# Streaming encoder step on one core: the gather of the sample heads in the bank of the transposes, the row sums on GpSimd, and a place of its own for one row tile

## The reference, cut to what matters

```
for l in range(2):
    p = rmsnorm(x, g_norm[l]) @ w_in[l]
    o_a = sparse attention (top 256 keys of an indexer), o_b = forgetting attention,
    o_c = chunk-band attention, o_m = cross-attention into 256 memory tokens   # 4 heads of 64 each
    x = x + concat(o * silu(own gate columns of p)) @ w_out[l]                 # 1024 x 1024
y = rmsnorm(x, g_final)
```

## Time and profile before

| | us |
|---|---|
| median of 3 runs | 1720.25 |
| the profiled execution | 1722.64 |
| its span | 1720.8 |
| PE busy in the span | 1664.0 |
| DVE busy | 1094.3 |
| ACT busy | 626.3 |
| POOL busy | 301.4 |

### The profile page before, as it was taken

The page is one execution under the profiler, slowest core; times in us unless marked ns, Lnnn a source line. Parts: engine busy times, 40 slices in busy tenths (PEclk is TensorE's granted clock), DMA queues, the critical chain, the costliest instruction groups (busy, mean ns, idle before and its releaser), DMA issues.

```text
span 1720.8 us, 28357 instructions
## 1 busy us (share of the span) xinstructions
PE 1664.0 (97%) x9815; PEld 1120.9 (65%) x9815; DVE 1094.3 (64%) x2845; ACT 626.3 (36%) x1509; POOL 301.4 (18%) x484
## 2 busy tenths in 40 slices
PE   9999999999999999999999999999999999998998
PEld 4466666766677755578754666666666777555886
DVE  5747887788777334465445288787887773335554
ACT  3532333323343444423134323343333434454221
POOL 1233321100000020313021423220000010204010
PEclk9999999999999999999999999999999999999999
DMA  9443323122222331102351523231233132411021
GB/s 327 157 161 103 126 93 141 38 80 105 68 106 96 108 107 51 68 25 77 114 173 55 171 74 126 90 141 41 78 108 102 70 120 89 118 34 68 1 98 74
DMA packets 46381, 171.32 MB, mean 100 GB/s; under 512 B 11472, under 2 KB 11952, under 8 KB 43040
## 3 DMA queue, kind: packets, MB, share of 16 engines
q1 hardware_dynamic: 29632, 130.68, 22.7%
q0 software_dynamic: 16608, 38.83, 6.9%
HBM read 141.83 MB, written 30.73 MB: 100 GB/s over the span
## 4 chain that ended last, share of the span: by engine, by line
PE 60%; DVE 28%; issue 4%; DMA 2%; ACT 2%; ACTq 2%; DVEq 2%; SPq 0%
PE psX L1096 30%; DVE lower L1554 14%; PE psX L1124 10%; PE psT L1009 6%; PE psS L1232 5%; PE psX L1299 4%; DVE work L1830 4%; DMA kv<-in_memT 2%; PE psS L1151 1%; ACTq L1445 1%; DVE gate L1634 1%; PE psX L1009 1%; DVE work L1828 1%; ACT work L1486 1%; DVE gate L1844 1%
## 5 line engine op out<-in xcount | busy, mean ns | idle before, releaser
L1096 PE MATMUL psX<-wring,hT 128*128 128x512 f32 (+2 forms) x1504 | 605.8, 545 | 5.1 <-ACT qT L1405 2.9
L1554 DVE TENSOR_SCALAR_CACHE_REDUCE lower<-sc,thr 128x640 uint8<-128x640 f32 (+5 forms) x462 | 407.3, 933 | 17.2 <-issue 9.3
L1096 PEld LDWEIGHTS psX<-wring,hT 128*128 128x128 f32 x1504 | 271.6, 191 | 221.6 <-issue 213.6
L1096 PE MATMUL psX<-hT,wring 128*128 128x256 f32 (+1 forms) x1600 | 329.0, 360 | 4.5 <-ACT gate L1444 3.6
L1486 ACT ACTIVATE work<-work,stat 128x256 f32<-128x256 f32 (+7 forms) x288 | 200.0, 694 | 315.7 <-DVEq L1833 313.0
L1096 PEld LDWEIGHTS psX<-hT,wring 128*128 128x128 f32 x1600 | 275.5, 191 | 36.9 <-issue 8.1
L1495 ACT COPY work<-psT 128x512 f32<-128x512 f32 (+2 forms) x352 | 156.7, 487 | 321.2 <-PE psT L1009 318.7
L1009 PEld LDWEIGHTS psT<-con,work 128*128 128x128 f32 x1080 | 122.6, 142 | 65.7 <-issue 54.2
L1009 PE MATMUL psT<-con,work 128*128 128x128 f32 x1080 | 160.0, 280 | 0.9 <-ACT kv L1454 0.9
L1830 DVE CUSTOM_DVE_ANT_0 work<-psS,bias 128x640 f32<-128x640 f32 (+7 forms) x120 | 86.2, 718 | 48.7 <-PE psT L1009 25.4
L1878 POOL DMA_DIRECT2D scratch_oscr<-gate x54 | 30.6, 567 | 363.0 <-DVEq L1864 296.5
(11 more groups left out here) (270 smaller groups left out, 1917.9 us busy)
## 6 DMA issues: line engine op xcount, KB each, us to landing
wring<-in_w SPq DMA_DIRECT2D x16, 2048.0 KB, 8.7
cache<-in_kB SPq DMA_DIRECT2D x16, 512.0 KB, 5.8
cache<-in_vB SPq DMA_DIRECT2D x16, 512.0 KB, 4.0
cache<-in_kC SPq DMA_DIRECT2D x16, 512.0 KB, 6.0
cache<-in_vC SPq DMA_DIRECT2D x16, 512.0 KB, 4.7
scratch_oscr<-gate POOLq DMA_DIRECT2D x54, 128.0 KB, 2.1
hT<-scratch_oscr SPq DMA_DIRECT2D x18, 384.0 KB, 3.0
kv<-in_x SPq DMA_DIRECT2D x9, 512.0 KB, 5.7
```

Source lines behind the costliest of these rows:

```text
L1096: mm = pe.matmul(out, lhs, rhs, start=(kt == 0), stop=(kt == KT - 1))
L1554: v.tensor_scalar(lower[:, at:at + STRIP_L[t]], sc[:, o], thr[:, n:n + 1], 0.0, ALU.is_lt, ALU.add, accum_out=below[:, n:n + 1])
```

## The change

Six things change:

1. `R` writes to `psT` in place of `psX`, as one more use in the turns.
2. `Sh` of pairs 0 and 1 moves from DVE to GpSimd. Both stand in the order as soon as the gathered samples and the values of the tiles are through, which is behind unit (A2, 6). The third sum of each pair is written over the row quarter that it reads; other sums change places, and `stage` is no longer one of them.
3. `Tw` of `O0` stands in the order as soon as the last samples of A and the last pack of M are through, which is behind unit (A2, 5), one unit earlier; it no longer waits for the scores of tile 5, and its third and fourth sums lie in `cache`. `Tw` of `O1` stands behind the first seven products of `O0` instead of ahead of them, waits for the scores of tile 5 and puts its third and fourth sums in `sc`. In layer 0 GpSimd's two stores of these products are ahead of it in the order.
4. Row tile 4 gets a place of its own, `stage` as one block of 1024 columns, and is loaded right behind `TR` of (A2, 7). The other tiles turn through the four places without it.
5. Of a pair, tile 2p is normalized ahead of tile 2p+1.
6. `R` no longer counts in `acc_slots`; since it always follows a `V`, the banks of the others stay as they are. The rule for two packs in the units of M1 and A2 is untouched.

```diff
@@ program_order
-            if (c, t) == ("A2", 6):
-                for i in range(4):
-                    emit("Tw", "O0", i)
+            taken = {s[1] for s in o if s[0] == l and s[1][0] in ("V", "GT")}
+            values_of = lambda t: ("V", packs_of("A", t)[-1]) in taken
+            for kind, at, due in (("Tw", "O0", ("V", ("A", "s3", 3, 1)) in taken and ("V", packs_of("M", NT - 1)[-1]) in taken),
+                                  ("Sh", 0, ("GT", "A") in taken and values_of(1)),
+                                  ("Sh", 1, ("GT", "A") in taken and values_of(3))):
+                if c == "A2" and due and (l, (kind, at, 0)) not in o:
+                    for i in range(4):
+                        emit(kind, at, i)
...
-                if c == "O0" and n < 4 and p < 2:
-                    emit("Sh", p, n)
...
+                    if (c, p) == ("O0", 0):
+                        for i in range(4):
+                            emit("Tw", "O1", i)
                 if c == "O1":
-                    to_norm += [p] if p == ST_ else [2 * p + 1, 2 * p]
+                    to_norm += [p] if p == ST_ else [2 * p, 2 * p + 1]
@@ with_loads
+    uses = [u for u in tile_uses(o) if not has_own_place(u)]
+    for l in range(DEPTH):
+        put(at[(l, ("TR", "A2", NT - 1))], l, "X", ("r", 4))
+def has_own_place(u):
+    return u[1] == ("r", 4)
@@ encoder
-            elif k in ("GT", "FT", "wsel"):
+            elif k in ("R", "GT", "FT", "wsel"):
                 t_uses.append((l, s))
...
+        xt.append(stage.rearrange("p a b -> p (a b)"))
...
+        w_sums = {"O0": [... (flat_q[:, 0:1024], flat_q[:, 1024:2048], cache[:, 0, :], cache[:, 1, :])],
+                  "O1": [... (cache[:, 2, :], cache[:, 3, :], sc[:, 0:1024], sc[:, 1024:2048])]}
+        row_sums = [[... (flat(mK[:, :, :]), flat(mV[:, :, :]), sbias_[:, 0:512])],
+                    [... (sc[:, SC_OFF[ST_]:SC_OFF[ST_] + 512], lower[:, 1024:].bitcast(F32), flat(om[:, :, :]))]]
@@ tensor, R
-                    pe.wait_ge(X.empty(s).sem, X.free(s))
+                    pe.wait_ge(T.empty(s).sem, T.free(s))
@@ vector
-                elif k == "Sh" and s[1] < 2:
-                    (four sums L1648, waits for the loaded rows)
@@ gpsimd, Tw
-                            pool.wait_ge(*X.fill(("V", last_m)).on(("V", last_m)))
+                            for use in (("V", last_m), ("V", last_sample["A"])):
+                                pool.wait_ge(*X.fill(use).on(use))
+                        else:
                             pool.wait_ge(*logits.on((packs_of("A", 5)[-1], 1)))
@@ gpsimd, Sh
+                        else:
+                            pool.wait_ge(*gated.on("A"))
+                            pool.wait_ge(*k_stored.on("mm"))
+                            pool.wait_ge(*v_stored.on(("mm", 1)))
+                            pool.wait_ge(*sm_stored.on("s"))
```

More of the change, by code:

```diff
@@ L715, in encoder @@
         stored_dmas = lambda c, t: 3 if c == "A1" else 0
-        tiles = tile_uses(order)
+        tiles = [u for u in tile_uses(order) if not has_own_place(u)]
         xt_slot = {u: n % XR for n, u in enumerate(tiles)}
         tile_loaded = [Signal(sem(f"tile{k}_loaded"), tiles[k::XR], lambda e: 16) for k in range(XR)]
+        placed = [u for u in tile_uses(order) if has_own_place(u)]
+        xt_slot.update({u: XR for u in placed})
+        tile_loaded.append(Signal(sem(f"tile{XR}_loaded"), placed, lambda e: 16))
+        xt.append(stage.rearrange("p a b -> p (a b)"))
         norms = events(["norm"], lambda s: s[1])
@@ L802, in encoder @@
         quarter = lambda ap: ap.rearrange("p (k c) -> p k c", k=KT // 2)
-        w_sums = {"O0": [quarter(ap) for ap in (flat_q[:, 0:1024], flat_q[:, 1024:2048], sc[:, 0:1024], sc[:, 1024:2048])],
-                  "O1": [quarter(cache[:, i, :]) for i in range(4)]}
+        w_sums = {"O0": [quarter(ap) for ap in (flat_q[:, 0:1024], flat_q[:, 1024:2048], cache[:, 0, :], cache[:, 1, :])],
+                  "O1": [quarter(ap) for ap in (cache[:, 2, :], cache[:, 3, :], sc[:, 0:1024], sc[:, 1024:2048])]}
         flat = lambda ap: ap.rearrange("p a b -> p (a b)")
-        row_sums = [[quarter(ap) for ap in (flat(mK[:, :, :]), flat(mV[:, :, :]), sc[:, SC_OFF[ST_]:SC_OFF[ST_] + 512], sbias_[:, 0:512])],
-                    [quarter(ap) for ap in (stage[:, 0, :], stage[:, 1, :], sc[:, SC_OFF[6]:SC_OFF[6] + 512],
-                                            lower[:, 0:2048].bitcast(F32))]]
+        row_sums = [[quarter(ap) for ap in (flat(mK[:, :, :]), flat(mV[:, :, :]), sbias_[:, 0:512])],
+                    [quarter(ap) for ap in (sc[:, SC_OFF[ST_]:SC_OFF[ST_] + 512], lower[:, 1024:].bitcast(F32),
+                                            flat(om[:, :, :]))]]
         def row_sum(p, i):
             upper, lower_ = hT[:, 2 * p, :, :], hT[:, 2 * p + 1, :, :]
-            s1, s2, s3, s4 = row_sums[p % 2]
+            s1, s2, s4 = row_sums[p % 2]
+            s3 = lower_[:, FIRST_LINES, :]
             return [(s1, lower_[:, FIRST_LINES, :], lower_[:, LAST_LINES, :], ALU.add),
@@ L1865, in _ @@
                 elif k == "R":
-                    dve.wait_ge(*X.fill(s).on(s))
+                    dve.wait_ge(*T.fill(s).on(s))
                     ga = gates(s[1])[:, ST_, :]
-                    v.tensor_tensor(ga, X.ap(s)[:, 0:W], ga, ALU.mult).then_inc(X.empty(s).sem, 1)
+                    v.tensor_tensor(ga, T.ap(s)[:, 0:W], ga, ALU.mult).then_inc(T.empty(s).sem, 1)
                     dve.drain().then_inc(gated.sem, 1)
@@ L1989, in _ @@
                     pool.drain()
-                elif k == "Sh" and s[1] >= 2:
+                elif k == "Sh":
                     p, i = s[1:]
                     if i == 0:
-                        use = ("G", "O1", p - 2, 6)
-                        pool.wait_ge(*X.fill(use).on(use))
+                        if p >= 2:
+                            use = ("G", "O1", p - 2, 6)
+                            pool.wait_ge(*X.fill(use).on(use))
+                        else:
[3 more added lines that the diff above has]
+                            pool.wait_ge(*sm_stored.on("s"))
                         for t in (2 * p, 2 * p + 1):
@@ L1999, in _ @@
                     g.tensor_tensor(*row_sum(p, i))
-                    pool.drain().then_inc(rows_combined[1].sem, 1)
+                    pool.drain().then_inc(rows_combined.sem, 1)
                 elif k == "G" and s[3] == 6:
```

36 lines of the change are left out of this document (10 added, 26 removed).

## The result

The changed kernel takes 1696.37 us, the median of four runs (1694.85 to 1697.39); the kernel before took 1719.84 beside it (four runs, 1718.79 to 1721.93). The ratio is 0.9861, with a 95% interval of 0.9844 to 0.9878: 23.5 us less, where 19.9 were forecast. The profiled execution has a span of 1694.1 us and a time of its own of 1695.91.

The account below looks back on a forecast made before the run. PE (TensorE) was taken to set the pace, busy 97% of the span with 56.8 us idle; 14.1 + 3.0 + 10.4 - 7.6 = 19.9 us off 1720.25 gave 1700.4 us, range 1688 to 1710.

Parts of the forecast that it names:

- B and C, forecast 14.1: Gathers of branches B and C: R in psT removes four waits and slow clock, adds shorter waits, net 14.1 us gained.
- M, 3.0: Gather of branch M: two waits of 1.52 us go with nothing in their place, 3.0 us gained.
- new waits at the transposes: Transposes behind R wait for DVE to empty R's bank: 0.8 us at B, 1.2 us at C.
- DVE gets to the values when it does whatever PE does: Gather of B: DVE, in its search rounds, reaches the values at 257.04 whatever PE does.
- The rival that DVE's search rounds are the bound there: Gathers of B and C: the 14.1 us come back as waits of scores or transposes, 1714.5 us; chance 0.15.
- A, forecast -7.6: Gather of A: weight sums on GpSimd hold DVE's rotation, losing 3.8 us a layer, 7.6 in all.
- The term of the clock, 1.6 us a layer: Gather of A: 1.6 us added for the slow clock behind an idle time of some 4 us.
- The rival that GpSimd misses the rotation: Gather of A: DVE's rotation goes ahead of GpSimd's sums, giving 1689.3 or 1692.8 us; chance 0.25.
- The row sums off DVE, forecast 10.4: First products G of each layer: five waits, 7.4 us, and layer 0's slow clock, 3.0 us, go; 10.4 us gained.
- the other five waits, 7.4 us: Waits of G in the first seven products of a layer, 7.4 of 8.8 us, claimed to go.
- The scalings can lose up to 1.27 us to each, but have some 3 us until PE asks for the result: DVE's scalings L1844 beside the eight GpSimd row sums, 692 to 704: up to 1.27 us held each, some 3 us spare.
- The edits taken at nothing: Tw of O1's new place, the load of tile 4 and normalizing 2p ahead of 2p+1: each counted as no time.

Follow-up runs that it names:

- e1: The kernel before with one edit, the gather R writing to psT in place of psX: 1698.99 us, ratio 0.9875.
- e3: The changed kernel with one more GpSimd wait: the weight sums Tw of O0 wait until the samples of A are gated; 1691.89 us, ratio 0.9837.
- e4: e3 with the first two weight sums of O0 put earlier, the other two still waiting for the gathered A: 1689.45 us, ratio 0.9821.
- e5: e4 with two more GpSimd waits: third weight sum behind the fifth tile's scaling, row sums of pair 1 behind the seventh tile's rotation; 1685.6 us, ratio 0.98.
- e9: e5 with the row sums of pair 1 also waiting for the scaling of the sixth tile's first pack: 1684.13 us, ratio 0.9794.
- e6: The changed kernel with row tile 4 of A2 back in one of the four rotating places: 1696.05 us, ratio 0.9856.
- e7: The changed kernel with the old order of norms within a pair, second tile first: 1695.11 us, ratio 0.9854.
- e2: The changed kernel with the gather R back in psX, so all edits but the bank: 1718.51 us, ratio 0.9988.
- e8: e5 with the gather R issued behind the next pack's transposes instead of ahead of them: 1689.45 us, ratio 0.9822.

## Why the prediction held, and where its sum was off

**B and C, forecast 14.1, and M, 3.0.** Measured in the table, 8.78 + 7.45 + 1.95 = 18.2 us for the three, against 17.1. In e1, with the bank alone, the same stretches give 16.9. Of the 1.3 us between the two, 0.36 is a wait for ACT in M of layer 1 (1.65 before, 1.64 in e1, 1.29 after); the others are small waits as well. The two steps are seen one by one: L1326 without a wait, a clock of 1.00 behind it, and new waits at the transposes, forecast 0.8 at B and 1.2 at C, of 0.58 and 1.14 in layer 0 and 0.22 and 1.33 in layer 1. The terms given for B add up to 0.6 rather than 0.8 (258.0 less 254.7 + 0.64 + 1.6 + 0.5). That DVE gets to the values when it does whatever PE does came true to the hundredth: 253.86 after and 257.04 before, with 3.18 us between the two traces already at 201. e1 shows it without the rest, 20.6 us with A's 3.5. The rival that DVE's search rounds are the bound there would have brought the waits back somewhere in 260 to 450. None came: the two waits of PE there, 0.56 and 1.05 us for ACT, are those of before (0.56 and 1.04). DVE had the room that the prediction read from its waits for PE, 5.3 us in 258 to 300 before and 1.8 us in the same work after.

**A, forecast -7.6.** Measured -4.92 - 3.28 = -8.2. The rotation was held twice, for 1.97 and 2.17 us, by the third and fourth sum, as worked out from the rows of before, and the wait behind it was 3.52 where some 4 were said. The term of the clock, 1.6 us a layer, was a middle value: by the windows it is (1 - 0.62) x 8 = 3.0 us in layer 0 and (1 - 0.79) x 8 = 1.7 in layer 1. The rival that GpSimd misses the rotation hung on 0.35 us; the third sum was 0.42 us ahead, in both layers. By the Trainium skill (SBUF — State Buffer, Who interferes with whom) issue order decides which of the two waits, for the whole of the other's instruction; what the prediction quotes beside it, that a VectorE instruction with at most one SBUF input does not contend, the page says of instructions outside VectorE's 2-port modes only. The timelines agree, to 0.03 us at the first group, and they show one thing more: a hold ends with the sum, but at the drain between the two groups of a rotation the next sum got in first, so the rotation was held twice. The same was seen at the seventh tile in e3, by 1.04 and 1.10 us; in e4, where the sum in question was the last, the first group took 0.61 us and the second 0.19.

**The row sums off DVE, forecast 10.4: the term that was mis-sized.** It measured 7.62 + 5.96 = 13.6 us, and with it the whole comes to 18.2 - 8.2 + 13.6 = 23.6. The step that fell short is that it counted "the other five waits, 7.4 us", and the slow clock. The slow clock was right, 3.1 us (3.75 + 3.15 us from start to start 3.54 + 2.99, less 2 x 1.73). The rest is more than the shown idle time. In layer 1, where no clock falls, the first four groups before took 1589.34 - 1577.32 = 12.0 us from start to start; the same four took 1564.43 - 1556.54 = 7.9 after. That is 4.1 us for waits of 0.22, 1.57 and 1.58 us in the profile, 3.4 in all: some 0.25 us a wait is missing. A group of eight lasts 1.89 us in the row and starts 1.73 behind the one ahead of it, so the row counts an overlap with that one's end; behind a wait there is none. Five waits in layer 1 and two in layer 0 give some 1.6 us, and the two waits of 0.22 us that were not in the count 0.4. Most of the rest are three gaps that the view does not list as waits: groups that started 1.97 or 1.98 us behind the one ahead, at 741.88, 753.73 and 1606.08, start 1.73 behind it in the changed kernel.

**"The scalings can lose up to 1.27 us to each, but have some 3 us until PE asks for the result"** was wrong as an argument, though no time was lost by it: in the changed kernel the scaling at 680.31 was held to 1.16 us while PE was late itself, at the low clock. e3 and e5 show that two of the three scalings have none to speak of: a hold of 2.05 us more (2.34 less 0.29) gave PE a wait of 1.83, and one of 0.68 a wait 0.68 longer. The one between them has about a microsecond (held by 0.99 in e3 at no cost). The list of what has two operands in SBUF, rotations and scalings, left out the gate L1634 (bias<-stage,bias); no sum stood ahead of it, and it took its 0.41 to 0.42 us in the changed kernel and in e3, e4, e5 and e9.

**The edits taken at nothing** were worth nothing in the median: e6 and e7 show two of them; Tw of O1 made no wait of PE in its new place.

**The 2.4 us between the profiled execution and the median**, left open in the prediction, are of the size of what executions differ by in the first 70 us, shown at the end; that it is this is not shown. The chance of the forecast itself, its range and the rivals were weighed on the mechanism, and the mechanism came; the forecast of 1700.4 lies 4.0 us above the result, 3.2 of them in the products G.

## What to carry to other kernels

A sum moved from a busy engine to an idle one is not free because the idle engine has time: lay its instructions out, one by one with their start times, beside those instructions of the other engine that a sum was seen to hold, here DVE's with both inputs in SBUF, and put each into a stretch where that engine reads PSUM or waits. Here that placing was worth 12 us (e3, e4, e5 and e9), half as much as the whole change. Where PE waits for a bank, ask whose bank it is and what stands next in the turn before the order is touched, and count a wait of a pipelined engine from start to start of its groups, not by the idle time alone.

## What the runs showed of the hardware

The first weight sum of a layer is followed by a pause of 3.12 us in which GpSimd waits for nothing that the profile shows, in the kernel before, in the changed one and in e3, wherever the sum stands; it belongs to the first sum and not to a place. Where the first two are put early it is 3.12 to 4.05 us long (3.44 and 3.12 in e4, 3.76 and 4.05 in e5, 3.80 and 3.31 in e9), and the third, 30 us later, has none (timeline of POOL in e5):

```profile
640.27 2.36 POOL L1999 TENSOR_TENSOR qT<-wring 128x1024 f32<-128x1024 f32 x1
646.39 2.36 POOL L1999 TENSOR_TENSOR qT<-wring,qT 128x1024 f32<-128x1024 f32 x1 [3.76 <-issue]
...
678.78 2.36 POOL L1999 TENSOR_TENSOR cache<-wring 128x1024 f32<-128x1024 f32 x1 [30.03 <-DVEq L1856]
681.30 2.36 POOL L1999 TENSOR_TENSOR cache<-wring,qT 128x1024 f32<-128x1024 f32 x1 [0.16 <-issue]
```

What it is was not tried.

An idle time of about the same length costs the clock differently: 3.52 us gave 0.62 in the next 8 us, and 3.53 us gave 0.79, in the two layers of one execution. Waits of 3.53 us gave 0.66 and 0.79 in e7 and 0.81 and 0.79 in e6. So the price of a wait this long is known to some 1.5 us only.

The traces differ in a stretch that has no edit. The timeline of PE in the changed kernel, then in e6, whose instructions there are the same:

```profile
67.46 1.56 PE L1169 MATMUL psS<-kA,qT 64*128 64x512 f32 x8 [0.59 <-ACT work L1495]
...
198.48 1.75 PE L1113 MATMUL psX<-hT,wring 128*128 128x256 f32 x7 [1.12 <-ACT gate L1462]
```

```profile
65.48 1.56 PE L1167 MATMUL psS<-kA,qT 64*128 64x512 f32 x8 [1.59 <-ACTq L1474]
70.92 1.56 PE L1167 MATMUL psS<-kA,qT 64*128 64x512 f32 x8 [1.39 <-ACT work L1493]
...
202.72 4.55 PE L1111 MATMUL psX<-hT,wring 128*128 128x256 f32 x20 [1.12 <-ACT gate L1460]
```

With the pair of waits at 65 and 71 the product comes at 201.7 to 202.7 (the kernel before, e2, e6), with one wait of about 0.6 us at 67 in their place at 197.9 to 199.2 (the changed kernel, e1, e3, e4, e7, e9); e5 and e8 lie between, at 200.2 and 199.5. A comparison of two spans carries up to 5 us of this. In e6 it is 4.2 us against the changed kernel, two waits of 0.54 and 0.80 us at 10 and 15 us among them. With the 1.76 us at 962, and less 1.5 us at the gather of A in layer 0, where the clock fell less, that is nearly all of the 4.7 us by which its span is the longer one, and of the distance of its 1700.57 us from its median of 1696.05. Each kernel has one trace, and what sets the stretch was not tried.
